# Two narrow matmuls become one wide one in a decoder's first layer, with the halves added on VectorE

## The reference

```python
# layer 0
h = rmsnorm(x, mixer_norm[0])
q1, q2, q3, k, v, qc = split_cols(h @ even_w_in[0], ...)   # 3 x 1024 | 1024 | 1024 | 256 columns
mix = mixer_dilated((q1, q2, q3), k, v, rel_bias)          # 16 heads, one softmax over three dilations
x = x + concat([mix, cross_attention(qc, mem_n, w_mem_kv[0])]) @ w_out[0]
h = rmsnorm(x, ffn_norm[0])
x = x + (silu(h @ w_gate) * (h @ w_up)) @ w_down           # width 2816
# layer 1
... sparse attention over chosen keys, cross attention, top-2-of-8 expert SwiGLU of width 3584
out = rmsnorm(x, final_norm)
```

## Time and profile before

| | |
|---|---|
| median of 3 runs | 1571.96 us (1570.99 to 1572.61) |
| profiled execution, own time | 1572.91 us |
| its span, first to last instruction | 1570.9 us |
| PE busy | 1532.5 us (98%) |
| DVE busy | 1310.0 us (83%) |
| ACT busy | 1115.9 us (71%) |
| mean granted TensorE clock | 0.991 |

### The profile page before, as it was taken

The page is one execution under the profiler, slowest core; times in us unless marked ns, Lnnn a source line. Parts: engine busy times, 40 slices in busy tenths (PEclk is TensorE's granted clock), DMA queues, the critical chain, the costliest instruction groups (busy, mean ns, idle before and its releaser), DMA issues.

```text
span 1570.9 us, 25833 instructions
## 1 busy us (share of the span) xinstructions
PE 1532.5 (98%) x8510; PEld 1308.7 (83%) x8510; DVE 1310.0 (83%) x1770; ACT 1115.9 (71%) x1461; POOL 79.8 (5%) x58
## 2 busy tenths in 40 slices
PE   8899999999998999999999999999999999999997
PEld 7899978999987877888888888888888888888886
DVE  5788867666658877998998998998998998998997
ACT  5555555444446768878878878878878878878875
POOL 1333100000000001000000000000000000000000
PEclk9999999999999999999999999999999999999999
DMA  9845526666613467999999999999999999999992
GB/s 271 214 139 143 160 82 189 193 191 178 173 41 81 147 220 281 409 388 373 390 391 353 396 387 355 391 394 355 393 389 356 387 396 354 395 389 353 399 384 114
DMA packets 226996, 455.38 MB, mean 290 GB/s; under 512 B 12848, under 2 KB 120512, under 8 KB 226944
## 3 DMA queue, kind: packets, MB, share of 16 engines
q1 hardware_dynamic: 222800, 439.52, 77.2%
q0 software_dynamic: 4144, 15.22, 3.8%
HBM read 445.52 MB, written 9.18 MB: 289 GB/s over the span
## 4 chain that ended last, share of the span: by engine, by line
PE 88%; DVE 5%; ACT 3%; DMA 2%; issue 1%; ACTq 0%; POOL 0%; DVEq 0%; POOLq 0%
PE ps L722 28%; PE ps L724 27%; PE ps L723 27%; PE ps L1124 2%; DMA big<-in_even_w_in 2%; PE ps L810 1%; ACT w_hi L1162 1%; DVE w_lo L1486 1%; PE ps L840 1%; DVE small L1573 1%; PE ps L825 1%; DVE z L1551 1%; DVE z L1570 1%; PE ps L1066 0%; ACT pr L1226 0%
## 5 line engine op out<-in xcount | busy, mean ns | idle before, releaser
L1486 DVE TENSOR_TENSOR w_lo<-big,w_hi 128x1024 fp32r<-128x1024 f32 (+1 forms) x843 | 987.8, 1209 | 183.6 <-ACT w_hi L1162 110.1
L1399 ACT CAST w_hi<-big 128x1024 fp32r<-128x1024 f32 x672 | 693.7, 1056 | 139.3 <-PE ps L724 136.3
L722 PE MATMUL ps<-w_hi,m_hi 128*128 128x512 f32 (+1 forms) x1008 | 391.9, 389 | 1.5 <-ACT qT L1217 1.3
L724 PE MATMUL ps<-w_hi,m_lo 128*128 128x512 f32 (+1 forms) x1008 | 389.4, 386 | 0.0
L723 PE MATMUL ps<-w_lo,m_hi 128*128 128x512 f32 (+1 forms) x1008 | 389.3, 386 | 0.0
L722 PE MATMUL ps<-h_hi,w_hi 128*128 128x256 f32 (+1 forms) x824 | 237.6, 288 | 4.5 <-DVE w_lo L1486 3.2
L723 PE MATMUL ps<-h_lo,w_hi 128*128 128x256 f32 (+1 forms) x824 | 233.5, 283 | 0.0
L724 PE MATMUL ps<-h_hi,w_lo 128*128 128x256 f32 (+1 forms) x824 | 233.4, 283 | 0.0
L722 PEld LDWEIGHTS ps<-w_hi,m_hi 128*128 128x128 f32 x1008 | 189.8, 188 | 41.3 <-issue 2.1
L724 PEld LDWEIGHTS ps<-w_hi,m_lo 128*128 128x128 f32 x1008 | 189.7, 188 | 38.3
L723 PEld LDWEIGHTS ps<-w_lo,m_hi 128*128 128x128 f32 x1008 | 189.8, 188 | 37.1
(11 more groups left out here) (262 smaller groups left out, 1268.8 us busy)
## 6 DMA issues: line engine op xcount, KB each, us to landing
big<-in_odd_w_gate SPq DMA_DIRECT2D x112, 1024.0 KB, 7.2
big<-in_odd_w_up SPq DMA_DIRECT2D x112, 1024.0 KB, 7.7
big<-in_odd_w_down SPq DMA_DIRECT2D x112, 1024.0 KB, 7.7
big<-in_even_w_in SPq DMA_DIRECT2D x42, 512.0 KB, 4.0
big<-in_even_w_gate SPq DMA_DIRECT2D x22, 512.0 KB, 3.8
big<-in_even_w_up SPq DMA_DIRECT2D x22, 512.0 KB, 3.9
big<-in_even_w_down SPq DMA_DIRECT2D x22, 512.0 KB, 4.2
big<-in_w_out SPq DMA_DIRECT2D x20, 512.0 KB, 3.6
```

The lines of the kernel that those rows point to most:

```text
L722: mm(dst, a[0], b[0], start=start, stop=False, **kw)
L724: return mm(dst, a[1], b[0], start=False, stop=stop, **kw)
L1399: nc.scalar.copy(w_hi[:, slot, :], ring[s][:, (u % 2) * UNIT:(u % 2 + 1) * UNIT]).then_inc(s_hi, 1)
L1486: return V.tensor_tensor(dst, src, lead.bitcast(F32), ALU.subtract)
```

## The change

`h_hi` and `h_lo` become the two halves of one tensor `h_two`, side by side for each chunk, so that both are one moving operand of 512 columns. A new `wide_product` replaces `product` in the 40 pair units of layer 0 and the 44 gate and up units: per chunk one matmul of 512 columns (high weights by both token parts) and one of 256 (low weights by high tokens): 16 matmuls for 24. The result is in two halves of a bank, which have to be added. ACT copies the second half to SBUF (`half` or `fcp`), and then DVE adds it to the first half. In the attention layer ACT's copy replaces its evacuation, and DVE's `halves` writes `qT`, `kT`, `vT` and counts `evacuated`. In the feed-forward ACT's `half_copy` and DVE's addition come on top; the multiplication that read PSUM now reads SBUF, and ACT's weight rounding moves ahead of SiLU. The diff, its core:

```diff
-        h_hi = sb("h_hi", [P, DC, SEQ], F32R)
-        h_lo = sb("h_lo", [P, DC, SEQ], F32R)
+        h_two = sb("h_two", [P, DC, 2, SEQ], F32R)
+        h_hi, h_lo = h_two[:, :, 0, :], h_two[:, :, 1, :]
...
+        fcp = (qflat[:, 768:1024], qflat[:, 1280:1536])
...
+        half = XH[:, 0, 0:512].rearrange("p (r n) -> p r n", r=2)
...
+            def wide_product(dst, w, norm=None):
+
+                for k in range(DC):
+                    if norm is not None:
+                        pe.wait_ge(s_nlo, DC * norm + k + 1)
+                    mm(dst, w[0][:, k, :], h_two[:, k, :, :].rearrange("p s n -> p (s n)"),
+                       start=k == 0, stop=k == DC - 1, skip_group_check=True)
+                    last = mm(dst[:, 0:SEQ], w[1][:, k, :], h_hi[:, k, :], start=False, stop=k == DC - 1,
+                              skip_group_check=True)
+                last.then_inc(s_used, 1)
+
             def project(pair, m, norm=None):
                 S = s_at[pair.l]
                 n = pair.before() + m
                 if not (isinstance(n, int) and n < 2):
-                    pe.wait_ge(S["evacuated"], n - 1)
+                    pe.wait_ge(S["evacuated"], pair_at(pair.l, PAIRS).before() if pair.cross else n - 1)
                 if pair.l == 0 and m == 0 and norm is None:
                     pe.wait_ge(S["third_read"], PAIRS if pair.cross else pair.g)
                 src, kc = (CS, RC) if pair.kind == "odd" and m > 0 else (HS, DC)
                 if src is CS:
                     pe.wait_ge(s_clo, RC)
                 w = split(pair.idx, pair.span[0], pair.unit(m), kc, width(pair, m))
+                if pair.kind == "even":
+                    wide_product(ps[:, pair.bank(m), :], w, norm)
+                    return
...
                 product(ps[:, pair.bank(m), 0:SEQ], w, src, kc, norm)
...
-                pe.wait_ge(S["evacuated"], pair.before() + (1 if pair.cross else pair.nbr + 1))
+                if pair.cross:
+                    pe.wait_ge(S["cross_queries"], pair.g - PAIRS + 1)
+                else:
+                    pe.wait_ge(S["evacuated"], pair.before() + pair.nbr + 1)
...
-                    pe.wait_ge(s_at[l]["evacuated"], pair_at(l, NPAIR - 1).before() + 1)
+                    pe.wait_ge(s_at[l]["cross_queries"], XPAIRS)
...
-                    if kind == "gate":
-                        pe.wait_ge(s_gr, c - 1)
-                    else:
-                        pe.wait_ge(s_fh, along(i, first, [2 * FFN[n][1] - 3 for n in ns]))
-                product(ps[:, (4 if kind == "gate" else 6) + par, 0:SEQ], w, HS, DC, norm)
+                    pe.wait_ge(s_gs if kind == "gate" else s_us, c - 1)
+                bank = (4 if kind == "gate" else 6) + par
+                wide_product(ps[:, bank, :], w, norm)
...
                 act.wait_ge(s_used, along(pair.idx, pair.span[0], [u + 1 for u in pair.unit(m)]))
+                if pair.kind == "even":
+                    n = pair.before() + m
+                    if not (isinstance(n, int) and n < 2):
+                        act.wait_ge(S["evacuated"], n - 1)
+                    nc.scalar.copy(half[:, (3 + pair.bank(m)) % 2, :], ps[:, pair.bank(m), SEQ:2 * SEQ]).then_inc(s_half, 1)
+                    return
...
-                nc.scalar.copy(dst, ps[:, pair.bank(m), 0:SEQ]).then_inc(S["evacuated"], 1)
+                nc.scalar.copy(dst, ps[:, pair.bank(m), 0:SEQ]).then_inc(S["cross_queries" if pair.cross else "evacuated"], 1)
...
+            def half_copy(i, first, ns):
+                kind, c0 = FFN[ns[0]]
+                if kind == "down":
+                    return
+                k = int(kind == "up")
+                act.wait_ge(s_used, along(i, first, [U.at[("ffn", n)] + 1 for n in ns]))
+                if c0:
+                    act.wait_ge((s_gs, s_us)[k], along(i, first, [FFN[n][1] for n in ns]))
+                nc.scalar.copy(fcp[k], ps[:, (4, 6)[k] + c0 % 2, SEQ:2 * SEQ]).then_inc((s_gc, s_uc)[k], 1)
...
             with act.Fori(1, FFN_LOOPS - 1) as i:
                 for k in range(6):
                     ns = [2 + 6 * b + k for b in span]
+                    half_copy(i, 1, ns)
+                    hi(i, 1, [after_unit(n) for n in ns])
                     silu(i, 1, ns)
-                    hi(i, 1, [after_unit(n) for n in ns])
...
+            def halves(pair, m):
+
+                S = s_at[0]
+                dve.wait_ge(s_half, pair.before() + m + 1)
+                if not (isinstance(pair.g, int) and pair.g < 2):
+                    dve.wait_ge(S["mixed"], 2 * pair.g - 1)
+                if m == pair.nbr + 1 and not (isinstance(pair.g, int) and pair.g < 1):
+                    dve.wait_ge(S["turned_v"], pair.g)
+                dst = qT[:, pair.par, m, :] if m < pair.nbr else kT[:, pair.par, :] if m == pair.nbr else vT[:, :]
+                V.tensor_tensor(dst, half[:, (3 + pair.bank(m)) % 2, :], ps[:, pair.bank(m), 0:SEQ],
+                                ALU.add).then_inc(S["evacuated"], 1)
...
+                def add(m):
+                    if now.gs[-1] < LATE:
+                        halves(nxt, m)
                 if now.kind == "even":
+                    add(0)
                     low(0)
+                    add(1)
                     low(1)
                     head_probs(now, 1)
+                    add(2)
                     low(2)
+                    add(3)
                     low(3)
                 else:
...
                     low(4)
+                    add(4)
...
                 for m in range(pair_at(l, 1).mats):
+                    if l == 0:
+                        halves(pair_at(l, 0), m)
                     lo_mat(pair_at(l, 1), m)
...
                 if kind == "gate":
                     if c0 >= 2:
                         dve.wait_ge(s_fs, c - 1)
-                    V.tensor_tensor(fgr[:, par, :], spread, ps[:, 4 + par, 0:SEQ], ALU.mult).then_inc(s_gr, 1)
+                    dve.wait_ge(s_gc, c + 1)
+                    V.tensor_tensor(fgr[:, par, :], fcp[0], ps[:, 4 + par, 0:SEQ], ALU.add).then_inc(s_gs, 1)
+                    dve.wait_ge(s_gs, c + 1)
+                    V.tensor_tensor(fgr[:, par, :], fgr[:, par, :], spread, ALU.mult).then_inc(s_gr, 1)
                     return
+                dve.wait_ge(s_uc, c + 1)
+                V.tensor_tensor(fh[:, par, :], fcp[1], ps[:, 6 + par, 0:SEQ], ALU.add).then_inc(s_us, 1)
+                dve.wait_ge(s_us, c + 1)
                 dve.wait_ge(s_fs, c + 1)
-                V.tensor_tensor(fh[:, par, :], fsg[:, par, :], ps[:, 6 + par, 0:SEQ], ALU.mult).then_inc(s_fh, 1)
+                V.tensor_tensor(fh[:, par, :], fh[:, par, :], fsg[:, par, :], ALU.mult).then_inc(s_fh, 1)
                 dve.wait_ge(s_fh, along(i, first, [2 * FFN[n][1] + 1 for n in ns]))
                 V.tensor_tensor(fh[:, par, :], fh[:, par, :], spread, ALU.mult).then_inc(s_fh, 1)
```

More of the change, by code:

```diff
@@ L368, in build @@
         esg, eh = qT[:, :, :, :].rearrange("p r b n -> p (r b n)")[:, 0:WIDE], pr[:, 0:WIDE]
-        e_hi = h_hi[:, :, :].rearrange("p c n -> p (c n)").rearrange("p (r k n) -> p r k n", r=2, k=WIDE // P)
-        e_lo = h_lo[:, :, :].rearrange("p c n -> p (c n)").rearrange("p (r k n) -> p r k n", r=2, k=WIDE // P)
+        e_all = h_two[:, :, :, :].rearrange("p c s n -> p (c s n)").rearrange("p (s r k n) -> p s r k n", s=2, r=2, k=WIDE // P)
+        e_hi, e_lo = e_all[:, 0, :, :, :], e_all[:, 1, :, :, :]
         g_hi = m_hi[:, 0:4, :].rearrange("p c n -> p (c n)").rearrange("p (c n) -> p c n", c=DC)
@@ L402, in build @@
         s_nma = sem("mean_square_part")
+        s_gs, s_us, s_gc, s_uc = map(sem, ("gate_summed", "up_summed", "gate_half_copied", "up_half_copied"))
         s_xrow, s_diag, s_rb, s_rbe, s_gr = map(
@@ L407, in build @@
         s_hi, s_lo, s_used = map(sem, ("unit_hi", "unit_lo", "unit_used"))
-        names = ("evacuated", "turned_v", "values", "scores", "scores_read", "masked", "max", "exp",
+        names = ("evacuated", "cross_queries", "turned_v", "values", "scores", "scores_read", "masked", "max", "exp",
                  "added", "summed", "third_left", "third_read", "probs", "probs_turned", "probsT", "mixed", "mix_hi", "mix_lo", "dve_rden")
@@ L411, in build @@
         s_me = sem("mem_evacuated")
+        s_half = sem("half_copied")
         s_fs, s_fh, s_fhi, s_fa = map(sem, ("ffn_silu", "ffn_hidden", "ffn_hidden_hi", "ffn_hidden_lo"))
@@ L741, in keep_warm @@
             def keep_warm(n, bank):
-                two = h_hi[:, 0:2, :].rearrange("p c n -> p (c n)")
+                two = h_two[:, 0, :, :].rearrange("p s n -> p (s n)")
                 for _ in range(n):
@@ L1343, in _ @@
             for n in range(8):
+                half_copy(0, 0, [n])
+                hi(0, 0, [after_unit(n)])
                 silu(0, 0, [n])
-                hi(0, 0, [after_unit(n)])
             span = range(1, FFN_LOOPS - 1)
@@ L1349, in _ @@
                     ns = [2 + 6 * b + k for b in span]
```

(6 more changed lines are left out.)

## The result

The changed kernel takes 1598.03 us (median; 1596.47 to 1599.95) against 1572.28 us for the kernel before in the same comparison: a ratio of 1.0163 (95% interval 1.0144 to 1.0182). It is slower by 25.8 us, the way that was forecast, and twice as far: the prediction was 1585 us, its range ended at 1590. The profiled execution took 1599.95 us by its own time, its span 1597.8 us.

What follows compares the result with a forecast made beforehand. The attention steps and the feed-forward were both taken as PE-bound. 0.5 + 9.8 + 3.5 + 1.7 - 2.4 = 13.1 us on 1572.9 gave 1586.0, the median 0.95 lower: 1585 us, range 1577 to 1590.

Steps and rivals of the forecast that it cites:

- first step: First attention step: only the addition ahead of the scores is newly in the way, scores 0.5 us later.
- six steps: Attention steps from the scores of pair 1 to those of pair 7: 1.64 us more each, 9.8 us in all.
- to the cross scores: First LATE step: first cross unit 3.5 us later, plus 1.7 us lost to the lower clock behind that wait.
- feed-forward: Gate and up units: 352 chunks gain 2.4 us (up to 4.4), DVE's additions and ACT's copies costed at 0.
- add 2: 0.34; lo 2 like lo 4, 143.33 - 142.20: 1.13: DVE's queue ahead of the scores: third of five additions 0.34 us, then third weight unit's subtraction 1.13 us.
- so there I add nothing: Clock inside the attention steps: new PE idle stretches of about 0.7 and 1.3 us cost no clock loss.
- the circle: Attention steps: PE and DVE wait for each other in a closed loop whose length, 20.51 us against 18.87, is the step.
- the half clock comes into the steps: Rival: two idle stretches per attention step lose 1.7 us in each of seven steps, 12 us more, 1597; chance 0.07.
- the wait of the first cross unit: First LATE step: the first cross unit waits for all 40 additions and begins 3.5 us later, PE idle meanwhile.
- the 1.7 us that were put in for it: Over the cross units: full-clock time lost to the lower clock behind the 3.5 us idle stretch, about 6 in 10.
- the two bounds of the prediction: Chunk time from wide-matmul rows: 0.3521 us with the feed-forward's own figure, 0.3464 with the experts', against 0.3588 before.
- Its cover: Feed-forward: additions and copies are not wanted soon, so cost 0; without that, about 0.8 us a unit.

Runs made afterwards that it cites:

- Experiment 3: The changed kernel with GpSimd's mask additions released when DVE has begun to read the scores, instead of by the probabilities; 1587.26 us, 1.0093.
- experiment 4: The changed kernel with 8 dummy matmuls of 512 columns put into PE's wait ahead of the scores; 1596.32 us, 1.0149.
- experiment 5: The kernel before, with only GpSimd's mask additions released later, when DVE has begun to read the scores; 1571.88 us, 0.9997.
- experiment 6: The changed kernel with the attention additions placed elsewhere in DVE's order, GpSimd's masks as in the changed kernel; 1580.04 us, 1.0047.
- Experiment 8: The changed kernel with additions reordered, GpSimd's masks released later, and the first pair's additions moved ahead of weight units in DVE's order; 1571.77 us, 1.0000.
- experiment 7: The changed kernel with both the attention additions reordered on DVE and GpSimd's masks released later; 1574.04 us, 1.0009.
- experiment 1: The change in the feed-forward alone, the attention layer computing as in the kernel before; 1567.43 us, 0.9970.
- experiment 2: The change in the attention layer alone, the feed-forward as in the kernel before; 1603.63 us, 1.0188.

## Why the prediction was wrong, and where it was right

Landmarks of the two profiled executions, predicted and measured, in us:

| term | predicted | measured |
|---|---|---|
| up to the scores of pair 0 (60.41 to 63.24) | 0 | +2.8 |
| first step (16.97 to 18.52) | +0.5 | +1.6 |
| six steps (113.04 to 135.20) | +9.8 | +22.2 |
| to the cross scores (18.67 to 23.81) | +5.2 | +5.1 |
| feed-forward (189.07 to 186.10) | -2.4 | -3.0 |
| behind it | 0 | -1.8 |
| span | +13.1 | +26.9 |

**The step that failed** is the line "add 2: 0.34; lo 2 like lo 4, 143.33 - 142.20: 1.13". Lo 2 took 2.22 us from start to start (123.78 to 126.00). I had looked at which engine waits for a semaphore, and the masks that GpSimd adds beside lo 2 are waited for only a step later; that two engines can hold each other up without a semaphore was not in the sum. Experiment 3 shows what hung on it: with the masks moved and nothing else, 10.8 us of the median go, the half clock among them. With it fell the sentence "so there I add nothing" on the clock: the rows allowed waits of up to 1.3 us, and the wait had become 2.1 on average. Split by steps: 18.84, then 20.58 with the circle alone (experiment 3; 1.74 us, 1.64 forecast), 21.56 with the exclusion (experiment 4; 0.98 us), 22.53 with the half clock (0.97 us). The first step shows the exclusion too: 18.52 us, and 17.41 in experiment 3, where 17.47 was forecast. Of the 13.8 us by which the span exceeds the forecast, the exclusion makes 7.0 (1.1 in the first step, 5.9 in the six), the half clock in the steps 5.8 and the start 2.8; the 1.8 us behind the feed-forward go the other way. The rival "the half clock comes into the steps" named the right second mechanism at 0.07, with layer 1's short waits as the argument against it; the argument was about waits of a size that these no longer had. Its figure, 1597 us, lies near the measured time by luck: it put 12 us down to the clock, which took 5.8, and had neither the exclusion nor the start.

The row that could have warned stood in the trace before: GpSimd's masks begin 0.27 us behind lo 2 and take 5.58 us for three, 1.86 us each, where experiment 3 has 1.26 us each. In the kernel before it was mainly GpSimd that was held up, and nobody waited for it (experiment 5). The Trainium skill, SBUF — State Buffer, section "Who interferes with whom", has the rule: a VectorE instruction with two SBUF inputs contends with a GpSimd instruction that reads SBUF, the ports that they share are an exclusive lock, and the order of issue decides which of the two blocks. The trace agrees: 2.29 us is the remaining 1.21 us of GpSimd's instruction and 1.08 of lo 2's own work. The additions themselves, with one operand in PSUM, stayed at 0.41 us beside GpSimd (add 3 at 126.00). The readings of the scores, which also have one operand in PSUM, kept their 0.41 us as well (experiments 3 and 6).

**The start** was not in the prediction. PE waited 1.6 us for add 0 behind a queue of weight units (the same kind of wait, in the code of the first pair; there four weight units of DVE take 8.95 us, with GpSimd busy beside them), and the mean granted clock from 46 to 53 us was 0.51 (0.76 in the kernel before). Experiment 8 brings the first scores back to within 0.65 us, in one profile of each and with the scatter given there. How the start's loss divides between queue, masks and clock was not separated.

**The circle** holds in its length, 20.51 us forecast and 20.58 in experiment 3, as does the wait of the first cross unit (3.6 us, 3.5 forecast) and what follows it:

```profile
227.00:233.00 6.00, 6.00 (x41) 6.00 (x40) 1.62 (x5) 1.59 (x3) 0.00 (x0) 0.72 0.27 87
```

Again a mean clock of 0.72 over 6 us, the 1.7 us that were put in for it at 6 in 10.

**The feed-forward** gained 3.0 us and not 2.4. Gate and up together take 5.65 and 5.55 us by turns where they took 5.74, so a chunk costs 0.353 or 0.347 us, 0.350 on average: about the two bounds of the prediction (0.3521 and 0.3464), one after the other. The 3.0 us are 3.2 from these units and 0.3 from the shorter wait ahead of the first down unit, less 0.5 that the down units take longer in all. Its cover held: no wait for a bank. The prediction set the Trainium skill's formula of columns over 2.4 GHz plus 2.5 ns beside this, as that of a stream; the section gives it there for the isolated gap of one matmul. It would have given 0.9 us; the measurement decides for the rows.

**Behind the feed-forward** 1.8 us are missing that no part of the change explains. They lie in one stretch, from layer 1's first normalised rows (L1533) to its residual (L1658); before and after:

```profile
439.37:586.71 147.34, 136.80 (x953) 114.57 (x954) 111.12 (x299) 86.39 (x217) 0.00 (x0) 0.98 0.39 124
```

```profile
467.87:613.36 145.49, 134.35 (x953) 112.23 (x954) 110.98 (x298) 86.40 (x217) 0.00 (x0) 1.00 0.40 125
```

The same instructions, the clock at 0.98 in the one and 1.00 in the other. Other profiled executions have the lower clock there or not without any edit near it (experiment 4 has it, 5 has not). I take it for chance between executions; it was not tested.

## What to carry to other kernels

Where work moves from an engine that runs ahead to one with an in-order queue, follow the queue around the whole loop: what stands before the new instruction, who waits for it, and whether that waiter feeds the queue's head again. If so, the new step is the length of that circle, however idle the engine is on average; here the order of five additions and three masks was worth 24 us, their load at most the 6.6 us that experiment 7 lies above experiment 1. And before inserting an instruction ahead of another, look at what GpSimd starts at that moment: 0.3 us decided here which of the two waited for the other. When a chain is lengthened, check each wait of the fast engine again for the clock, since one correction (1.1 us more) moved these waits over the size that the old trace had shown to be harmless.

## What the runs showed of the hardware

- VectorE's subtraction with both operands in SBUF (1.22 us) and GpSimd's addition (1.27 us) exclude each other in either order: 2.29 us for the one when GpSimd began 0.06 us ahead of it, 5.58 us for three of GpSimd's when VectorE was ahead. Moving GpSimd behind restored 1.22 us, and so did the one step without masks.
- TensorE's waits of 1.3 us left the granted clock at full in six steps (experiment 3), and so did those of 1.73 and 1.90 us in the first step of the changed kernel and of experiment 2. Waits of 2.3 to 2.4 us were followed by 0.50, the 1.2 GHz level, for part or all of the scores in five of five steps of the changed kernel (2.91 to 3.90 us for 2.24) and in three of five of experiment 2. Filling the wait with dummy matmuls kept the clock in all steps.
- One matmul of 512 columns and one of 256 by turns cost 0.350 us a pair on average over 44 units, a little less than the sum of 0.2325 and 0.1196 us that each costs in a row of its own kind.
